# Attention of the two layers: values in column strips with turned outputs, negated logits, gates in the scaling, four logits buffers

## The reference

```python
# x: (256, 1024); h = x @ w_in, split
o_a = mla_mixer(...)     # 8 heads of 64: causal softmax(q k^T * 96**-0.5) @ v
o_b = nsa_mixer(...)     # 8 heads of 64, gates = sigmoid(gate_logits), per head 3:
#   p_c = masked_softmax(q kc^T * scale - slope * distance)   over 15 compressed keys
#   p_s, p_w: the same over the selected blocks and the window (at 256 positions: all causal keys)
#   out = gate0 * p_c @ vc + gate1 * p_s @ vs + gate2 * p_w @ vw
mix = concatenate([o_a, o_b]) @ w_out
x = layer_norm(ALPHA * x + mix)
x = layer_norm(ALPHA * x + memory_cross_attn(x, ...))   # 4 heads of 256 over 256 memory rows
x = layer_norm(ALPHA * x + conv_ffn(x))
```

## Time and profile before

| | |
|---|---|
| three runs, median | 1696.79 us (1696.77 to 1696.97) |
| the profiled execution | 1696.81 us, of it span 1694.9 us |
| busy: PE, DVE, ACT, POOL | 1665.5, 1223.2, 352.5, 212.7 us |
| mean granted TensorE clock | 0.998 |
| attention of the layers, first run of the code | about 831 to 892 us |
| second run | about 1312 to 1373 us |

### The profile page before, as it was taken

How to read it: one execution, slowest core, us unless ns; L and a number is a source line. 1 busy time by engine, 2 the same in 40 slices (tenths; PEclk the granted TensorE clock), 3 DMA queues, 4 the chain that set the end, 5 groups by cost and what they waited for, 6 DMA issues and landing times.

```text
span 1694.9 us, 22817 instructions
## 1 busy us (share of the span) xinstructions
PE 1665.5 (98%) x8726; PEld 1281.4 (76%) x8726; DVE 1223.2 (72%) x2230; ACT 352.5 (21%) x893; POOL 212.7 (13%) x139
## 2 busy tenths in 40 slices
PE   7999999999999999999999999999999999999998
PEld 6887488877847886477784969994687767699953
DVE  6777467976787777573376778996844685789995
ACT  2111000034511111112270212220012531222210
POOL 1222211121021212211001000002120000000021
PEclk9999999999999999999999999999999999999999
DMA  9685454524176555346513536444447206265440
GB/s 320 194 230 177 146 199 162 175 80 149 51 232 213 160 164 184 124 145 178 207 51 131 155 125 194 156 170 153 158 121 252 100 1 224 71 226 177 150 173 25
DMA packets 163755, 267.07 MB, mean 158 GB/s; under 512 B 4279, under 2 KB 106477, under 8 KB 163519
## 3 DMA queue, kind: packets, MB, share of 16 engines
q1 hardware_dynamic: 157902, 248.66, 43.8%
q0 software_dynamic: 5008, 15.91, 3.3%
q10 hardware_dynamic: 736, 1.05, 0.3%
HBM read 262.52 MB, written 2.03 MB: 156 GB/s over the span
## 4 chain that ended last, share of the span: by engine, by line
PE 90%; DVE 5%; DVEq 2%; issue 1%; ACT 1%; DMA 1%; SPq 0%; ACTq 0%
PE psum L1017 19%; PE psum L886 16%; PE psum L1065 13%; PE psum L952 12%; PE psum L844 7%; PE psum L1275 4%; PE psum L1481 3%; PE psum L1538 3%; PE psum L1190 3%; PE psum L1116 3%; PE psum L1232 2%; PE psum L825 2%; PE psum L1104 2%; PE psum L1206 1%; PE psum L1221 1%
## 5 line engine op out<-in xcount | busy, mean ns | idle before, releaser
L695 POOL TENSOR_TENSOR work<-ring,work 128x1024 f32<-128x1024 f32 (+2 forms) x59 | 147.4, 2499 | 791.5 <-DVE work L2199 791.5
L2191 DVE TENSOR_TENSOR work<-ring 128x1024 f32<-128x1024 f32 (+2 forms) x102 | 122.0, 1196 | 83.3 <-PE psum L1065 74.3
L1065 PE MATMUL psum<-ring,work 128*128 128x512 f32 x352 | 160.8, 592 | 0.0
L2195 DVE TENSOR_TENSOR ring<-ring 128x1024 f32<-128x1024 f32 (+2 forms) x104 | 131.7, 1267 | 7.7
L2199 DVE TENSOR_TENSOR work<-ring 128x1024 f32<-128x1024 f32 (+2 forms) x102 | 122.6, 1202 | 7.6
L1065 PEld LDWEIGHTS psum<-ring,work 128*128 128x128 f32 x352 | 66.4, 190 | 81.1 <-issue 79.9
L1065 PE MATMUL psum<-work 128*128 128x512 f32 x264 | 122.5, 592 | 0.0
L1017 PE MATMUL psum<-x_t,work 128*128 128x128 f32 x832 | 101.4, 275 | 0.0
L1017 PE MATMUL psum<-work,ring 128*128 128x128 f32 x832 | 101.4, 275 | 0.0
L1017 PE MATMUL psum<-x_t,ring 128*128 128x128 f32 x832 | 97.4, 275 | 1.6 <-ACT x_t L1610 1.6
L1017 PEld LDWEIGHTS psum<-x_t,work 128*128 128x128 f32 x832 | 97.1, 192 | 0.0
(11 more groups left out here) (304 smaller groups left out, 2865.6 us busy)
## 6 DMA issues: line engine op xcount, KB each, us to landing
ring<-in_ffn_w_up_dram SPq DMA_DIRECT2D x66, 1024.0 KB, 7.9
ring<-in_w_in_dram SPq DMA_DIRECT2D x21, 2048.0 KB, 7.9
ring<-in_ffn_w_down_dram SPq DMA_DIRECT2D x20, 2048.0 KB, 7.8
ring<-in_ffn_w_gate_dram SPq DMA_DIRECT2D x22, 1024.0 KB, 5.7
ring<-in_xa_wkv_dram SPq DMA_DIRECT2D x8, 2048.0 KB, 9.5
ring<-in_w_out_dram SPq DMA_DIRECT2D x6, 2048.0 KB, 10.9
ring<-in_xa_wq_dram SPq DMA_DIRECT2D x4, 2048.0 KB, 7.9
ring<-in_xa_wo_dram SPq DMA_DIRECT2D x4, 2048.0 KB, 11.3
```

What stands on the lines that cost most here:

```text
L695: nc.gpsimd.tensor_tensor(t4, quarters(n, chunks, pitch)[2], t2, ALU.subtract).then_inc(fourth_ready, 1)
L1065: last = mm(sums[p], acts[p][:, q, :], rhs[:, i, :], start=(q == 0), stop=(q == KF // 2 - 1))
L2191: v.tensor_tensor(t3, b22, b12, ALU.subtract)
L2195: v.tensor_tensor(b12, b12, b11, ALU.subtract)
```

## The change

- S, W and M units are scaled on the probabilities in `mid` (kinds "BKSWMX"): reciprocal, then each head's probabilities times the reciprocal, for S and W in the same operation times the gate. K's `mid` takes reciprocal, gate and scaling too. `output` does nothing more for them.
- `turned_values` has 64 value columns stationary and the turned probabilities moving. The two heads of a unit write to partitions 0 to 63 and 64 to 127, in turn. K, S and W of one tile accumulate into one PSUM bank, M into another. The values of two units, S with W and M with M, are issued together at the second. K has four products of 128 columns.
- ACT copies finished banks into `XT` (`turned_rows_out`), twice per tile. The batches `E_O` and `turn_mixed` are gone; `shared_product` waits on `unit_done`.
- For S, W, M and X, `logits` computes minus score minus bias with a running minimum straight into `NM`; the negation and its drain are gone, and ACT's exponential has the scale -1.
- `attend` has a depth `ahead`: 3 for `UNITS_2`, with a fourth logits buffer in the space of `O1`; 2 elsewhere.
- K of tile 1 comes behind tile 0's units.

```diff
-UNITS_2 = [unit("K", 0, i) for i in range(TT)] + \
-          [x for i in range(TT) for x in [unit(k, h, i) for h in range(4) for k in "SW"] + [unit("M", h, i) for h in range(4)]]
+UNITS_2 = [x for i in range(TT) for x in
+           [unit("K", 0, i)] + [unit(k, h, i) for h in range(4) for k in "SW"] + [unit("M", h, i) for h in range(4)]]
+SPARSE_UNITS, TILE_UNITS = 9, 13
...
-            return w(W_L + 512 * (u % 3), 512)
+            if x["kind"] == "X":
+                return w(W_L + 512 * (u % 3), 512)
+            return w((W_L, W_L + 512, W_L + 1024, W_O1)[u % 4], 512)
...
+                def turned_values(j):
+                    x, u = units[j], u0 + j
+                    k = x["kind"]
+                    if k == "K":
+                        if x["tile"]:
+                            pe.wait_ge(unit_done, at(U1 + SPARSE_UNITS, U2, l))
+                        for c in range(4):
+                            last = mm(PO[:, c * P:(c + 1) * P], VBD[:, c // 2, (c % 2) * P:(c % 2 + 1) * P],
+                                      PTS[:, u % 2, (c // 2) * P:(c // 2 + 1) * P], start=(c == 0), stop=False)
+                        last.then_inc(values_ready, 1)
+                        return
+                    if k == "M" and x["tile"] and x["n"] == 1:
+                        pe.wait_ge(unit_done, at(U1 + TILE_UNITS, U2, l))
+                    for t in (j - 1, j):
+                        y = units[t]
+                        o = (512 if k == "M" else 0) + P * y["n"]
+                        for kb in range(y["nk"]):
+                            for s in range(2):
+                                n = s * y["nk"] + kb
+                                last = mm(PO[HD * s:HD * s + HD, o:o + P], values(y, s, kb), PTS[:, (u0 + t) % 2, n * P:(n + 1) * P],
+                                          start=(k == "M" and y["n"] == 0 and kb == 0), stop=(y["kind"] != "S" and y["n"] == 3 and kb == y["nk"] - 1))
+                    last.then_inc(values_ready, 2)
...
-                for j in range(n + 3):
+                for j in range(n + ahead + 1):
                     if j in between:
                         between[j]()
                     if j < n:
                         scores(j)
-                    if 0 <= j - 2 < n:
-                        turn(j - 2)
+                    if 0 <= j - ahead < n:
+                        turn(j - ahead)
...
-                    if 0 <= j - 3:
-                        value(j - 3)
+                    if 0 <= j - ahead - 1:
+                        value(j - ahead - 1)
...
-                shared_product(L_OUT, F_LOUT + F_LAYER * l, A_LOUT + A_LAYER * l, E_O, turn_mixed(E_O, U1 + TT + 12, 19, l), l)
+                shared_product(L_OUT, F_LOUT + F_LAYER * l, A_LOUT + A_LAYER * l, "O", lambda i: None, l)
...
-                            last = activation(v, v, ACT.Exp, bias=NM[:, b4, s:s + 1], accum_out=SM[:, b4, s:s + 1])
+                            last = activation(v, v, ACT.Exp, scale=-1.0 if x["kind"] in "SWMX" else 1.0, bias=NM[:, b4, s:s + 1],
+                                              accum_out=SM[:, b4, s:s + 1])
...
+                def turned_rows_out(j):
+                    x, u = units[j], u0 + j
+                    act.wait_ge(values_ready, at(u + 1, U2, l))
+                    i, sparse = x["tile"], x["kind"] == "W"
...
+                        copy(dst, src).then_inc(unit_done, SPARSE_UNITS if sparse else TILE_UNITS - SPARSE_UNITS)
...
-                turned_rows(E_O, XT, l)
...
-                    if j >= 3:
-                        dve.wait_ge(probs_turned, at(u - 2, U2, l))
+                    if j > ahead:
+                        dve.wait_ge(probs_turned, at(u - ahead, U2, l))
...
+                            if x["kind"] in "SWMX":
+                                last = v.tensor_tensor_reduce(out=dst, in0=src, in1=bias_of(x, s), scale=-1.0, scalar=-TAKEN,
+                                                              op0=ALU.add, op1=ALU.min, accum_out=NM[:, b4, s:s + 1])
...
+                        dr()
+                        v.reciprocal(RC[:, b4, :], SM[:, b4, :])
+                        dr()
+                        v.tensor_tensor(RC[:, b4, :], RC[:, b4, :], ngate[:, x["tile"], 0::3], ALU.mult)
+                        dr()
+                        v.tensor_tensor(L3, L3, RC[:, b4, :, None].to_broadcast([P, 8, NC]), ALU.mult).then_inc(mixed_ready, 1)
...
+                    if x["kind"] in "SW":
+                        c = 3 * 2 * x["n"] + (1 if x["kind"] == "S" else 2)
+                        for s in range(2):
+                            last = v.tensor_scalar(L[:, s * n:(s + 1) * n], L[:, s * n:(s + 1) * n], RC[:, b4, s:s + 1],
+                                                   ngate[:, x["tile"], c + 3 * s:c + 3 * s + 1], ALU.mult, ALU.mult)
+                        last.then_inc(mixed_ready, 1)
+                        return
...
-                    if 0 <= j - 1 < n and j != mid_first:
-                        mid(j - 1)
+                    if 0 <= j - ahead + 1 < n and j != mid_first:
+                        mid(j - ahead + 1)
...
-                attend(UNITS_2, U1, l)
+                attend(UNITS_2, U1, l, ahead=3)
...
-                act_sums_of(at(E_O + 4, B_LAYER, l))
+                act_sums_of(at(U1 + len(UNITS_2), U2, l), unit_done)
```

More of the change, by code:

```diff
@@ L230, in unit @@
     return dict(kind=kind, n=n, tile=tile, keys=keys, subs=subs, pitch=512 if kind == "C" else keys, nk=1 if kind == "K" else keys // P,
-                wide=kind == "A", mid=kind in "BKX")
+                wide=kind == "A", mid=kind in "BKSWMX")
 UNITS_1 = [unit("B", h, i) for i in range(TT) for h in range(4)] + \
@@ L1178, in values, with attend @@
                 return KV[:, kb, c:c + HD]
-            def attend(units, u0, l=None, between={}, behind_turn={}):
+            def attend(units, u0, l=None, between={}, behind_turn={}, ahead=2):
                 def scores(j):
@@ L1224, in value @@
                         return
-                    dv = P if k == "B" else T if k == "K" else HD
-                    blocks = [(s, kb) for s in range({"B": 1, "K": 2}.get(k, x["subs"])) for kb in range(x["nk"])]
+                    dv = P if k == "B" else HD
+                    blocks = [(s, kb) for s in range({"B": 1}.get(k, x["subs"])) for kb in range(x["nk"])]
                     for n, (s, kb) in enumerate(blocks):
@@ L1555, in _ @@
                 pe.wait_ge(key_shift, at(32, 32, l))
[L1556 removed]
+                attend(UNITS_2, U1, l, {1 + 2 * i + h: values_between(i, h) for i in range(TT) for h in range(2)}, ahead=3)
                 pe.wait_ge(group_free, at(H_WV + 2, G_LAYER, l))
[L1558 removed]
+                shared_product(L_OUT, F_LOUT + F_LAYER * l, A_LOUT + A_LAYER * l, "O", lambda i: None, l)
                 pe.wait_ge(share_in, 4 * l + 4)
@@ L1676, in first_copies, with attend @@
                 hidden(UPS - 1)
-            def attend(units, u0, l=None, between={}, behind_copy={}):
+            def attend(units, u0, l=None, between={}, behind_copy={}, ahead=2):
                 def exps(j):
@@ L1714, in mixed_rows @@
                         copy(dst, src).then_inc(unit_done, 1)
+                def turned_rows_out(j):
+                    x, u = units[j], u0 + j
+                    act.wait_ge(values_ready, at(u + 1, U2, l))
+                    i, sparse = x["tile"], x["kind"] == "W"
+                    src = PO[:, 0:512] if sparse else PO[:, 512:1024]
+                    src = src.rearrange("p (k t) -> p k t", k=4)
+                    dst = XT[:, 4:8, i * P:(i + 1) * P] if sparse else XT[:, 0:4, i * P:(i + 1) * P]
+                    if not sparse and i == 0:
+                        copy(dst[:, 0:2, :], src[:, 0:2, :]).then_inc(quarter_out, 1)
+                        copy(dst[:, 2:4, :], src[:, 2:4, :]).then_inc(unit_done, TILE_UNITS - SPARSE_UNITS)
+                    else:
+                        copy(dst, src).then_inc(unit_done, SPARSE_UNITS if sparse else TILE_UNITS - SPARSE_UNITS)
                 n = len(units)
-                for j in range(n + 4):
+                for j in range(n + ahead + 2):
                     if j in between:
                         between[j]()
-                    if 0 <= j - 2 < n:
-                        out_of_psum(j - 2)
+                    if 0 <= j - ahead < n:
+                        out_of_psum(j - ahead)
                     if j in behind_copy:
@@ L1727, in attend @@
                         mixed_rows(j - 3)
+                    if 0 <= j - ahead - 1 < n and units[j - ahead - 1]["kind"] in "WM" and units[j - ahead - 1]["n"] == 3:
+                        turned_rows_out(j - ahead - 1)
             def evacuate(n, j, g, dst, width, l=None):
@@ L2320, in bias_of, with attend @@
                 return zero_bias[:, 0:x["keys"]]
-            def attend(units, u0, l=None, between={}, mid_first=None):
+            def attend(units, u0, l=None, between={}, mid_first=None, ahead=2):
```

62 lines of the change are left out of this document (25 added, 37 removed).

## The result

| | us | against before (95% interval) |
|---|---|---|
| before, median of 9 runs | 1696.79 (1696.48 to 1698.17) | |
| after, median of 9 runs | 1701.27 (1701.04 to 1702.78) | 1.0026 (1.0018 to 1.0035) |
| forecast | 1697.1, range 1684 to 1705 | 1.0002 |

What follows compares the result with a forecast made beforehand. TensorE, busy 98% of 1694.9 us, was taken to bound the kernel, with waits on VectorE's scaling giving back the savings. From 1696.8, +0.3 per layer in attention and -0.15 per layer in memory attention, both twice, gave 1697.1; range 1684 to 1705.

Steps and rivals of the forecast that it cites:

- the walk: The prediction's step-by-step timing of layer 0's attention, from 847.78 to 894.4 against 894.09 before: +0.3 us per layer.
- step 6: Tile 0, first layer: PE waits for the scaling of S1, then turns and values, ending at 852.07.
- step 14: Around tile 1's K: DVE does K's logits, then the scaling of unit 11; PE waits 1.1, end 864.16.
- step 16: Around tile 1's K: K's scaling waits for the logits of step 15; PE waits 1.6, end 868.64.
- step 19: Tile 1, after K: logits, scalings, turns and a value burst of 0.95, ending at 875.14.
- drain: End of the attention loop, a chain of ACT copies, exponentials and last values with nothing beside it: 6.44 us.
- the burst of 64 instructions: Compressed keys' four 32-column strips in the earlier trace: 1.88 us, 1.71 of it bare, 0.17 left for all overheads.
- the third rival: Each change of strips waits for PE's tail: 2.8 us more per layer, 1702.6 us; chance 0.12.
- PE's own work sets the pace: Attention: DVE and ACT run ahead, depth hides all; 11.8 us less per layer, 1673 us; chance 0.10.
- Strips don't overlap: Value pairs: no overlap at 64 columns, 6.5 us more per layer, 1710 us; chance 0.05.
- DVE's chain is longer: Two-value scaling at 0.42 and left-out hand-overs at semaphores: 2 us more per layer, 1701 us; chance 0.06.
- The bounds: Uncertainty of strips' price, two-value scaling and hand-overs: together about 2 us per layer, 4 in all, 1693 to 1701.

Runs made afterwards that it cites:

- run 1: Changed kernel with DVE's scaling of unit j-2 put ahead of the logits of unit j, instead of behind: 1686.61 us, 0.9938.
- run 8: Changed kernel with a depth of 2 instead of 3 on all three engines, nothing else: 1701.49 us, 1.0026.
- run 7: Changed kernel with plain logits, running maximum and the negation with its drain put back for S, W, M and X: 1707.18 us, 1.0061.
- run 3: Changed kernel with all values of a pair for partitions 0 to 63 first, then all for 64 to 127: 1707.36 us, 1.0061.
- Run 4: Changed kernel with the gate left out of the scaling of S and W units, so scaled by the reciprocal alone: 1700.08 us, 1.0019.
- run 9: Kernel with scaling ahead of logits, four copy buffers and late sparse rows, but two steps deep instead of three: 1726.55 us, 1.0173.

## Why the prediction was nearly right, and where it failed

**The mechanism** came as the walk had it. PE waits ahead of every second turn in tile 1, ended by the scaling; two longer waits stand around the second K; ACT releases the last two bursts; there are no transposes behind attention. Runs 1 and 8 show that it is the order on DVE, run 7 that each 0.24 of DVE's time in a pair is 0.24 of the pair, run 3 the same of the values.

**The sizes.** Ends of the steps by the walk and in the timeline of after:

| end of | walk | after | drift |
|---|---|---|---|
| step 6 | 852.07 | 852.27 | +0.2 |
| three pairs, tile 0 | 860.26 | 861.37 | +1.1 |
| step 14 | 864.16 | 865.56 | +1.4 |
| step 16 | 868.64 | 870.19 | +1.6 |
| step 19 | 875.14 | 876.88 | +1.7 |
| three pairs, tile 1 | 887.92 | 890.28 | +2.4 |
| drain | 894.4 | 896.41 | +2.0 |

The last pair of them in the timeline of PE, after:

```profile
889.25 1.09 PE L1233 MATMUL psum<-work 128*64 128x128 f32 x16
890.28 0.66 PE L1210 MATMUL psum<-ident_fours,work 128*128 128x128 f32 x4
```

Most of the drift grows pair by pair (0.9 in three pairs of tile 0, 0.7 in three of tile 1), so the step that failed is the sum of a pair, four of its terms:

- *Scores behind a burst*: walk 0.92 and 0.44; after 876.88 to 877.85 = 0.97 and 852.27 to 852.82 = 0.55.
- *Turns ahead of a burst*: walk 0.50 and 0.28; after 875.27 to 875.86 = 0.59 and 854.48 to 854.85 = 0.37. The first turn of the X units, with no strips behind it, takes the 0.50 of the earlier trace rows in after too (966.94 to 967.44). So 0.09 belongs to entering the strips.
- *Values*: walk 0.95 and 0.53; after 875.86 to 876.88 = 1.02 and 854.85 to 855.43 = 0.58.
- *Two-value scaling*: walk 1.63 and 1.23 for DVE's stretch; after 878.05 to 879.72 = 1.67 and 856.18 to 857.45 = 1.27. Two errors hide each other in it. The scalings themselves took 0.74 and 0.60, where the walk had 0.62 and 0.50; but the walk put 0.08 for the last read of the accumulator ahead of the reciprocal, and the two start together (878.75). Run 4 prices the second value at 0.6 per layer; the prediction's bound said 0.5.

The first three are one thing: I laid all that the burst of 64 instructions left over bare cost into the burst itself, and the instructions on either side at their old price. A burst of tile 1 costs (1.02 - 0.86) + 0.05 + 0.09 = 0.30 over bare, one of tile 0 (0.58 - 0.43) + 0.11 + 0.09 = 0.35, where the walk had 0.09 and 0.10. That is the price which the third rival named, 0.32 in each of 12 pairs. It came to less than its 1702.6, because, by the walk, the bursts that fall under the memory blocks do not all push the end, and because the drain was 6.13 and not 6.44.

Luck has a share in the small distance: the drain came 0.3 shorter per layer than the walk had it, and the scaling's excess was partly covered by the read of the accumulator. Without these two the forecast would have missed by more than the 4.2 us that it did.

The Trainium skill, page TensorEngine Tiling (Array Packing), section Tiling Modes, says that changing the tiling mode drains TensorE. By that rule a cost at both ends of each burst is to be expected; the 0.05 to 0.11 on one side and 0.09 on the other agree with it in kind, and no run here shows whether a drain is what they are.

**The rivals.** "PE's own work sets the pace", 1673, was the nearest description of what the same work can do in another order. Its pair of 3.65 became 3.83 in run 1: the difference is 0.18 in the bursts and their neighbours. What kept the prediction from it, the order of DVE's queue, held. "Strips don't overlap" fell by run 3. "DVE's chain is longer" was right by 0.6 of its 2 per layer.

**The chances** were the weak spot. The bounds were summed to 1693 to 1701, and the measured 1701.27 lies at their upper end. The scaling stood at the low end of its bounds (0.35 of 0.35 to 0.42), the burst in the middle of its own (0.95 of 0.86 to 1.03), and what a burst does to the instructions on either side at nothing. A loop where every term lies on one path adds up misses of the same sign, so faster should have had less than slower.

**Readings that were off** without weight in the sum: the terms of a tile-1 pair add up to 4.25, not 4.26; and of the 12.2 us that PE shows from 850 to 863 not half but some 2.8 us are tails, as PE needs 1.09 of each 1.51, 9.4 of 13 us.

**Open:** why the two scalings of one tile-0 unit of the first layer take 0.74 (853.68) where the others take 0.60, which makes the pair from 852.27 to 855.43 3.16 long and not 3.03; and whether the 0.4 of wait that run 1 keeps at the second K can go, which was not tried.

## What to carry to other kernels

When steps are made deeper on one engine, look on every in-order queue at what stands ahead of the old unit's step: the work of the newest unit there cancels the depth, and putting the oldest first was worth 14.7 us here without removing an instruction. Price a burst in another tiling at both its ends as well as by its length, and count it once per burst, not once per instruction. Where all terms of a loop lie on one path, small misses add up; spread the chances by the sum of the bounds.

## What the runs showed of the hardware

- A burst of 8 to 16 fp32 instructions of 128 columns in 64-column strips costs 0.30 to 0.35 us over its bare time (an estimate: bare time is half of 0.107 for each instruction): 0.16 in itself, 0.05 to 0.11 on what follows, 0.09 on what is ahead.
- Two strips overlap with four instructions of one ahead of four of the other (0.60 against 0.59), and only partly with eight ahead of eight (1.51; in turns 1.02; without any overlap 16 x 0.107 + 0.16 = 1.87). The 0.36 saved is some three instructions, so the second strip seems to start about that much early; that is worked out from one length and not measured by more.
- A scaling of 128x256 fp32 by two per-partition values takes 0.41 us (0.74 for two), by one 0.35 (0.62 for two).
- In run 9, where PE waits most, the granted clock fell to 0.50, its 1.2 GHz level, three times around the attention of the two layers. The view by windows of that kernel, PE (length, busy, clock, DMA share, GB/s), the end of attention in the first layer and, in the last row, the same place in the second:

```profile
900.00:905.00 5.00, 2.95 (x28) 0.97 0.01 3
905.00:910.00 5.00, 3.57 (x25) 0.50 0.00 0
910.00:915.00 5.00, 5.00 (x10) 0.85 0.00 0
1400.00:1405.00 5.00, 2.34 (x24) 1.00 0.00 0
```

PE was idle for 2.05 of the first five us; then 0.50 was granted, and the last burst of 16 values took 1.91 (907.94 to 909.85) instead of 1.02. In the second layer, behind the same wait of 2.05 us, the clock stayed at 1.00 and the burst took 1.02 (1405.33 to 1406.35). So one long wait alone did not decide it. The other two falls came near the end of tile 0, with no wait above 1.1 us: PE was busy for 6.88 of the 10 us from 850, and from 864 to 870 0.50 was granted; in the second layer it was busy for 5.3 of the 8 us from 1350, and 0.50 was granted from 1360 to 1368. At that level scores of tile 0 took 1.01 (864.07 to 865.08) instead of 0.55. What tells the stretches that lose the clock from those that keep it stays open. In the changed kernel, with waits below 1.5 us, it stayed at 1.00 from 850 to 910.
